# A two-block transformer kernel: 512-column up products, down products two tiles behind, and zero-padded rope scores

## What is computed

```python
h = x                                        # [256, 1024]
for i in range(2):                           # mixer 0 is MLA, mixer 1 is differential attention
    a = mixer_i(rms_norm(h, norm_g[i, 0]))
    h = h + rms_norm(a, norm_g[i, 1])
    f = conv_ffn(rms_norm(h, norm_g[i, 2]), ffn_w_up[i], ...)
    h = h + rms_norm(f, norm_g[i, 3])

def conv_ffn(x, w_up, conv_w, conv_b, w_down):   # w_up [1024, 2*2816], w_down [2816, 1024]
    u = x @ w_up
    c = conv_b + sum over j of conv_w[j] * (u shifted by j-1 tokens)     # 3 taps along the tokens
    g, val = halves of c
    return (gelu(g) * val) @ w_down

# MLA scores, 8 heads:  q_nope (128) . k_nope (128)  +  q_rope (64) . k_rope (64)
```

## Time and profile before

| what | value |
|---|---|
| time, median of 3 runs | 1247.5 us (1238.12 to 1247.79) |
| profiled execution, its own time | 1248.45 us |
| span of the profiled execution | 1246.6 us |
| PE busy | 1195.6 us, 96% |
| DVE busy | 762.8 us, 61% |
| ACT busy | 599.7 us, 48% |
| chain that ended last, PE's share | 85% |
| moved from memory | 192.84 MB, 156 GB/s over the span |

### The profile page before, as it was taken

One profiled execution on the slowest core, in us unless ns is written; L12 is line 12 of the kernel. 1 busy time (PEld: TensorE's weight loads), 2 busy tenths in 40 slices (PEclk: granted clock), 3 DMA queues, 4 the chain that ended last, 5 costly groups with the idle time before them and its releaser, 6 DMA issues.

```text
span 1246.6 us, 21628 instructions
## 1 busy us (share of the span) xinstructions
PE 1195.6 (96%) x8061; PEld 1068.2 (86%) x8075; DVE 762.8 (61%) x1066; ACT 599.7 (48%) x912; POOL 66.7 (5%) x93
## 2 busy tenths in 40 slices
PE   7999999999898989999999999999999999999997
PEld 6856999999698869999988999998887777999996
DVE  4854877776656558777767545546555556554554
ACT  5444554454555655545545443435554545443342
POOL 0201000000200010000001000001000210000000
PEclk9999999999999999999999999999998899999998
DMA  6404665666343347566655666653762014766661
GB/s 219 155 34 152 187 198 175 183 199 197 102 136 136 126 123 206 174 181 202 182 155 139 199 191 178 187 160 86 201 224 102 1 35 136 204 199 182 174 183 43
DMA packets 241059, 194.61 MB, mean 156 GB/s; under 512 B 11214, under 2 KB 223792, under 8 KB 241008
## 3 DMA queue, kind: packets, MB, share of 16 engines
q1 hardware_dynamic: 240928, 193.88, 51.8%
q10 hardware_dynamic: 80, 0.03, 0.0%
HBM read 192.84 MB, written 1.05 MB: 156 GB/s over the span
## 4 chain that ended last, share of the span: by engine, by line
PE 85%; DVE 7%; ACT 3%; DMA 2%; issue 1%; POOL 1%; SPq 0%; POOLq 0%; ACTq 0%; DVEq 0%
PE psum L572 25%; PE psum L573 25%; PE psum L574 25%; DVE lo_u L1629 1%; PE psum L1130 1%; DVE lo_u L1646 1%; ACT hi_u L1223 1%; DMA raw_u<-in_cmp_v_w 1%; PE psum L804 1%; PE psum L803 1%; PE psum L917 1%; DVE soft L1850 1%; PE psum L1087 1%; DMA raw_u<-in_mla_w_ukv 1%; DMA raw_u<-in_cmp_k_w 1%
## 5 line engine op out<-in xcount | busy, mean ns | idle before, releaser
L572 PE MATMUL psum<-act_hi,hi_u 128*128 128x256 f32 x1712 | 487.6, 285 | 7.8 <-DVE lo_u L1629 3.2
L574 PE MATMUL psum<-act_hi,lo_u 128*128 128x256 f32 x1712 | 484.9, 283 | 0.0
L573 PE MATMUL psum<-act_lo,hi_u 128*128 128x256 f32 x1712 | 484.8, 283 | 0.0
L1646 DVE TENSOR_TENSOR lo_u<-raw_u,hi_u 128x2048 fp32r<-128x2048 f32 (+3 forms) x122 | 273.7, 2243 | 244.5 <-ACT hi_u L1229 153.0
L572 PEld LDWEIGHTS psum<-act_hi,hi_u 128*128 128x128 f32 x1712 | 327.3, 191 | 16.2 <-issue 12.4
L573 PEld LDWEIGHTS psum<-act_lo,hi_u 128*128 128x128 f32 x1712 | 327.4, 191 | 3.3
L574 PEld LDWEIGHTS psum<-act_hi,lo_u 128*128 128x128 f32 x1712 | 327.4, 191 | 0.0
L1229 ACT ACTIVATE hi_u<-raw_u 128x2048 fp32r<-128x2048 f32 x72 | 137.7, 1912 | 88.6 <-PE psum L574 86.0
L572 PE MATMUL psum<-hi_d,hid_hi 128*128 128x512 f32 (+1 forms) x352 | 138.4, 393 | 1.4 <-DVE hid_lo L1736 1.4
L573 PE MATMUL psum<-lo_d,hid_hi 128*128 128x512 f32 (+1 forms) x352 | 138.0, 392 | 0.0
L574 PE MATMUL psum<-hi_d,hid_lo 128*128 128x512 f32 (+1 forms) x352 | 137.0, 389 | 0.0
(11 more groups left out here) (230 smaller groups left out, 1234.8 us busy)
## 6 DMA issues: line engine op xcount, KB each, us to landing
raw_u<-in_ffn_w_up SPq DMA_DIRECT2D x88, 512.0 KB, 5.5
raw_d<-in_ffn_w_down SPq DMA_DIRECT2D x86, 512.0 KB, 3.5
raw_u<-in_ffn_w_gu SPq DMA_DIRECT2D x84, 512.0 KB, 5.9
raw_u<-in_diff_w_qkv SPq DMA_DIRECT2D x24, 512.0 KB, 4.6
raw_u<-in_w_in SPq DMA_DIRECT2D x24, 512.0 KB, 4.0
raw_u<-in_mla_w_o SPq DMA_DIRECT2D x8, 512.0 KB, 3.7
raw_u<-in_diff_w_o SPq DMA_DIRECT2D x8, 512.0 KB, 3.7
raw_u<-in_w_out SPq DMA_DIRECT2D x8, 512.0 KB, 3.9
```

Of the source, the lines that this page charges most:

```text
L572: pe.matmul(o, s_hi, m_hi, start=start, stop=False)
L573: pe.matmul(o, s_hi, m_lo, start=False, stop=False)
L574: return pe.matmul(o, s_lo, m_hi, start=False, stop=stop)
L1646: dve.tensor_tensor(v[0], v[1], v[2].bitcast(F32), ALU.subtract).then_inc(S("lo_u_done"), 1)
```

## The change

- **Up products.** The hi and lo parts of the activations now lie side by side in `act_hl`. One 512-column matmul computes hi*hi and hi*lo at once into the two halves of a bank, and one 256-column matmul adds lo*hi to the second half (`mm_beside`). A block step is two matmuls in the place of three. The sum of the two halves is now formed outside PE: ACT copies the second half out (`cross_out`), DVE adds it to the first (`sum_up`), for the gate and for the value. What follows reads `up_sum` in SBUF and not PSUM.
- **Order on PE.** `down(t)` now runs behind `up(t+2)`, where it ran behind `up(t+1)`. At the end of an FFN the four half blocks of tiles 20 and 21 alternate.
- **Order on ACT and DVE.** The down rows that are split in a tile's turn are other ones: before, turn t split rows t+1 on both engines; now ACT splits rows t at the end of turn t, and DVE forms the lo part of rows t-1 near the start of turn t, behind the first `sum_up`. The fp32r copy of the hidden product moves from DVE to ACT, and its lo part moves into the next turn of DVE. A third slot of `hi_d` and `lo_d` holds the rows of tile 21.
- **MLA.** `m_qr` and `m_kr` get 128 partitions; the upper 64 are set to zero by two memsets at the program's start, and L804 becomes a matmul with 128 rows.
- SP's program and POOL's are the same as before.

```diff
-        act_hi = sb("act_hi", [P, KC, SEQ], F32R)
-        act_lo = sb("act_lo", [P, KC, SEQ], F32R)
+        act_hl = sb("act_hl", [P, KC, 2, SEQ], F32R)
+        act_hi, act_lo = act_hl[:, :, 0, :], act_hl[:, :, 1, :]
...
-        hi_d = sb("hi_d", [P, 2, 1024], F32R)
-        lo_d = sb("lo_d", [P, 2, 1024], F32R)
+        hi_d = sb("hi_d", [P, 3, 1024], F32R)
+        lo_d = sb("lo_d", [P, 3, 1024], F32R)
...
+        cross = ar(2048, 2, 2, SEQ)
+        up_sum = ar(3072, 2, 2, SEQ)
+        def d_slot(d):
+            return 2 if d % FT == FT - 1 else d % 2
...
-        m_qr = ar(2048, H, SEQ, p=ROPE)
+        m_qr = ar(2048, H, SEQ)
...
-        m_kr = ar(8192, SEQ, p=ROPE)
+        m_kr = ar(8192, SEQ)
...
+            def mm_beside(bank, n, s_hi, s_lo, m_hl, start, stop):
+                pe.matmul(psum[0:n, bank, :], s_hi, m_hl.rearrange("p a t -> p (a t)"), start=start, stop=False)
+                return pe.matmul(psum[0:n, bank, SEQ:], s_lo, m_hl[:, 0, :], start=False, stop=stop)
...
-                        if f < 2:
-                            pe.wait_ge(S("tap_b"), g * 2 - 2)
-                        else:
-                            pe.wait_ge(S("hid_hi_done"), g - 1)
+                        pe.wait_ge(S("up_sum"), g * 2 - 2)
...
-                        mm = mm3(psum[0:n, 4 + 2 * slot + s, 0:SEQ], hi[:, k, :], lo[:, k, :],
-                                 act_hi[:, k, :], act_lo[:, k, :], k == 0, k == KC - 1)
+                        mm = mm_beside(4 + 2 * slot + s, n, hi[:, k, :], lo[:, k, :], act_hl[:, k],
+                                       k == 0, k == KC - 1)
                         if k == KC - 1:
                             mm.then_inc(S("gate_up" if s == 0 else "used_u"), 1)
...
                 up(1, 1, P)
-                down(0, 0, P)
                 with pe.Fori(0, LOOPED) as b:
                     up(b * 2 + 2, 0, P)
+                    down(b * 2, 0, P)
+                    up(b * 2 + 3, 1, P)
                     down(b * 2 + 1, 1, P)
-                    up(b * 2 + 3, 1, P)
-                    down(b * 2 + 2, 0, P)
                 up(20, 0, P)
+                down(18, 0, P)
+                up(21, 1, width(f, 21))
                 down(19, 1, P)
-                up(21, 1, width(f, 21))
-                down(20, 0, P)
+                down(20, 0, P, False, [0])
                 down(21, 1, width(f, 21), True, [0])
+                down(20, 0, P, False, [1])
                 down(21, 1, width(f, 21), True, [1])
...
+                pe.wait_ge(S("m_rope_zeros"), 2)
...
+                    def cross_out(part):
+                        if n < P or part:
+                            act.wait_ge(S("used_u"), at(u + 1))
+                        else:
+                            act.wait_ge(S("gate_up"), at(g + 1 - (f == 3)))
+                        act.activation(cross[:, slot, part, :], psum[:, 4 + 2 * slot + part, SEQ:], ACT.Copy)\
+                            .then_inc(S("cross_out"), 2 if n < P else 1)
+                    def conv_mid(part, buf):
+                        act.wait_ge(S("up_sum"), at2(2 * g + part + 1))
...
+                    cross_out(0)
+                    if f < 2:
+                        conv_mid(0, cg)
+                        cross_out(1)
+                        act.wait_ge(S("tap_b"), at2(2 * g + 1))
+                        act.activation(gg[0:n, slot, :], cg[0:n, slot, :], ACT.Gelu_apprx_tanh).then_inc(S("gated"), 1)
+                        conv_mid(1, cv)
                     else:
...
+                        act.wait_ge(S("up_sum"), at2(2 * g + (2 if n < P else 1)))
                         r = slice(n, 2 * n) if n < P else slice(0, P)
...
+                        act.activation(gg[r, slot, :], up_sum[0:n, slot, 0, :], ACT.Silu).then_inc(S("gated"), 1)
+                        if n == P:
+                            cross_out(1)
                     if b is not None:
                         split_u_looped(b, u + 2)
                     elif t < 20:
                         split_u(u + 2)
...
-                        split_d(g + 1, b)
-                split_d(FT * f)
+                    act.wait_ge(S("hidden"), at(g + 1))
+                    if b is not None or g >= 2:
+                        act.wait_ge(S("used_d"), at(g - 1))
+                    act.activation(hid_hi[0:n, slot, :], hf[0:n, slot, :], ACT.Copy).then_inc(S("hid_hi_done"), 1)
+                    if t + 1 < FT:
+                        split_d(g, b)
+                    if t == 20:
+                        split_d(g + 1)
...
+                slot = d_slot(d) if b is None else d % 2
                 dve.wait_ge(S("hi_d_done"), d + 1 if b is None else b * 2 + (d + 1))
-                dve.tensor_tensor(lo_d[:, d % 2, :], raw_d[:, d % 2, :], hi_d[:, d % 2, :].bitcast(F32),
+                dve.tensor_tensor(lo_d[:, slot, :], raw_d[:, d % 2, :], hi_d[:, slot, :].bitcast(F32),
                                   ALU.subtract).then_inc(S("lo_d_done"), 1)
...
+                    def sum_up(part):
+                        last = n < P
+                        dve.wait_ge(S("cross_out"), at2(2 * g + (2 if last else part + 1)))
+                        dve.tensor_tensor(up_sum[:, slot, part, :], psum[:, 4 + 2 * slot + part, 0:SEQ],
+                                          cross[:, slot, part, :], ALU.add).then_inc(S("up_sum"), 2 if last else 1)
+                    def taps(part, buf):
+                        for tap, name in ((0, "tap_a"), (2, "tap_b")):
+                            dve.wait_ge(S("conv_mid" if tap == 0 else "tap_a"), at2(2 * g + part + 1))
...
+                    def hidden_low(x, slot, n):
+                        dve.wait_ge(S("hid_hi_done"), at(x + 1))
+                        dve.tensor_tensor(hid_lo[0:n, slot, :], hf[0:n, slot, :], hid_hi[0:n, slot, :].bitcast(F32),
+                                          ALU.subtract).then_inc(S("hid_lo_done"), 1)
+                    sum_up(0)
+                    if b is not None or 0 < t < 21:
+                        split_d(g - 1, b)
                     if f < 2:
...
+                        taps(0, cg)
+                    if n == P:
+                        sum_up(1)
+                    if b is not None or t:
+                        hidden_low(g - 1, 1 - slot, P)
+                    dve.wait_ge(S("gated"), at(g + 1))
+                    if f < 2:
+                        taps(1, cv)
+                        dve.wait_ge(S("tap_b"), at2(2 * g + 2))
...
+                    dve.tensor_tensor(hf[0:n, slot, :], gate, val, ALU.mult).then_inc(S("hidden"), 1)
                     if b is not None or t < 20:
                         split_u(u + 2, b)
...
-                        split_d(g + 1, b)
-                split_d(FT * f)
+                    if t == 20:
+                        split_d(g)
+                        split_d(g + 1)
+                    if t == 21:
+                        hidden_low(g, slot, n)
...
+            dve.memset(m_qr[ROPE:], 0.0).then_inc(S("m_rope_zeros"), 1)
+            dve.memset(m_kr[ROPE:], 0.0).then_inc(S("m_rope_zeros"), 1)
```

More of the change, by code:

```diff
@@ L336, in program @@
         d_sq = junk[:].rearrange("p (b d) -> p b d", d=P)
-        d_hi, d_lo = (x[:].rearrange("p a (c t) -> p (a c) t", t=SEQ) for x in (hi_d, lo_d))
+        d_hi, d_lo = (x[:, 0:2].rearrange("p a (c t) -> p (a c) t", t=SEQ) for x in (hi_d, lo_d))
         n_q = ar(0, 4, SEQ)
@@ L691, in down @@
                     g = t + FT * f
+                    d = 2 if isinstance(t, int) and t == FT - 1 else slot
                     pe.wait_ge(S("hi_d_done"), g + 1)
@@ L699, in down @@
                             mm = mm3(psum[:, 2 * tk + c, :], hid_hi[0:n, slot, tok(tk)], hid_lo[0:n, slot, tok(tk)],
-                                     hi_d[0:n, slot, w], lo_d[0:n, slot, w], False, last)
-                    mm.then_inc(S("used_d" if TT - 1 in tiles else "first_part"), 1)
+                                     hi_d[0:n, d, w], lo_d[0:n, d, w], False, last)
+                    if TT - 1 in tiles:
+                        mm.then_inc(S("used_d"), 1)
+                    elif last:
+                        mm.then_inc(S("first_part"), 1)
                 up(0, 0, P, True)
@@ L1236, in split_d @@
                 elif d >= 2:
-                    act.wait_ge(S("used_d"), d - 1)
-                act.activation(hi_d[:, d % 2, :], raw_d[:, d % 2, :], ACT.Copy).then_inc(S("hi_d_done"), 1)
+                    act.wait_ge(S("used_d"), d - 1 - (d % FT == FT - 1))
+                act.activation(hi_d[:, d_slot(d) if b is None else d % 2, :], raw_d[:, d % 2, :], ACT.Copy)\
+                    .then_inc(S("hi_d_done"), 1)
             def norm(i):
@@ new lines, in tile @@
+                    if n == P:
[6 more added lines that the diff above has]
+                        dve.wait_ge(S("tap_b"), at2(2 * g + 2))
+                        gate, val = gg[0:n, slot, :], cv[0:n, slot, :]
+                    else:
```

(12 more changed lines are left out.)

61 lines of the change are left out of this document (16 added, 45 removed).

## The result

| | before | after |
|---|---|---|
| median | 1244.4 us (4 executions, 1238.1 to 1247.8) | 1635.0 us (4 executions, 1630.2 to 1641.4) |
| ratio, 95% interval | | 1.316 [1.312, 1.320] |
| profiled execution, its own time | 1248.45 us | 1630.16 us |
| span | 1246.6 us | 1628.4 us |
| FFN 0, first `up` to last `down` | 189.1 us | 287.9 us |

The changed kernel is 31.6% slower. From the page of the changed kernel: the engines, the chain that ended last by engine, two of the costliest groups (busy, mean ns | idle before, releaser) and two kinds of transfer.

What follows compares the result with a forecast made beforehand. PE bounds the kernel before, at 8.5 us a tile; after the change a ring through the load does, at 13.6 us. 1248.45 + 401 (FFNs) - 5.5 (MLA) + 1 (later stages) = 1645 us, 8 in 10 within 1580 to 1715.

Steps and rivals of the forecast that it cites:

- head: Stretch of each FFN ahead of the first round, from the first `up` through the first `lo_d`: about 15 us.
- one round: From one `lo_d` end to the next in the FFN loop: 13.6 us per tile, 18 rounds per FFN.
- tail: Stretch of an FFN behind `lo_d` of rows 18: 29 us in FFN 0 and 1, 26 us in 2 and 3.
- the four FFNs' growth: Time added to the FFNs together: 2 x 99.9 + 2 x 100.4 = 401 us.
- stages behind the FFNs: Stages after the FFNs get their loads later, since SP reaches them behind down rows 21: 0 to 3 us.
- The ring: FFN loop: `lo_d`, load, up unit's splits, `sum_up` and the next `lo_d` in series, 13.6 us per tile.
- The weighing of the transfers: FFN loads: 7.6 us from SP's issue until the up unit lands, preferred over a page's 5.6 us estimate.
- Loads in time: Rival: the FFN loads come in time and the kernel is faster, 1233 us; chance 0.05.
- Quicker load: Rival: the load is quicker when less else goes on, ring about 1.3 us shorter, 1551 us; chance 0.08.
- Slow clock: Rival: PE's clock falls to 1.2 GHz and PE becomes the bound, 15.4 us a tile, 1775 us; chance 0.05.
- I take the upper: Up products: of bounds 0 and 17.5 us of PE time saved, 17.5 was chosen, outside the sum.
- 347 ns in turns: Sign in PE's up products: a 512- and a 256-column matmul in turns take 347 ns, where three took 360.

Runs made afterwards that it cites:

- number 1: The changed kernel with SP's order alone altered, the up unit of tile t+1 issued ahead of the down rows of tile t: 1231.8 us, ratio 0.991.
- number 7: The kernel before with one edit on DVE, lo of down rows t-1 formed near the start of turn t: 1725.0 us, ratio 1.389.
- number 10: number 1 again with more executions, on the chip of number 9: 1229.3 us, ratio 0.990.
- number 5: The changed kernel with the second transfer of each looped up unit cut to one of its eight row blocks: 1515.9 us, ratio 1.220.
- number 4: The changed kernel, loads in its own order, with the block step of three 256-column matmuls: 1632.8 us, ratio 1.317.
- number 2: number 1 with the 512-column product split in two, so three 256-column products per block step: 1236.1 us, ratio 0.995.
- number 9: number 1 with the eight 512-column products of a gate or value first, then its eight 256-column ones: 1223.7 us, ratio 0.984.
- number 6: The changed kernel with ACT and DVE splitting down rows t inside turn t, ahead of the split of unit t+2: 1356.5 us, ratio 1.092.

## Why the prediction was right

The forecast was 1645 us, the profiled execution took 1630.2, and its mechanism was shown from both sides: taking the late `lo_d` out of the load's way removes the loss (number 1), and putting it there makes the loss in the kernel before (number 7). PE's timeline of the changed kernel in FFN 0, then in FFN 3, gives their lengths, 287.9 and 283.7 us:

```profile
121.67 0.47 PE L584 MATMUL psum<-act_hl,hi_u 128*128 128x512 f32 x1 [0.31 <-DVE act_hl L1702]
...
409.15 0.39 PE L580 MATMUL psum<-hi_d,hid_lo 128*128 128x512 f32 x1
...
1336.88 0.47 PE L584 MATMUL psum<-act_hl,hi_u 128*128 128x512 f32 x1 [0.31 <-DVE act_hl L1702]
...
1620.20 0.39 PE L580 MATMUL psum<-hi_d,hid_lo 64*128 64x512 f32 x1
```

Term by term, for FFN 0 where it isn't said otherwise:

| term | predicted | measured |
|---|---|---|
| head, first `up` to the end of the first `lo_d` | 15 us | 136.71 - 121.67 = 15.0 us |
| one round | 13.6 us | (379.75 - 136.94) / 18 = 13.5 us |
| of it, `raw_d` issued to `hi_u` started | 7.7 us | 7.2 and 7.5 us in the two turns shown, 7.6 in the mean of 18 |
| tail | 29 us | 409.54 - 379.68 = 29.9 us |
| FFN 0, FFN 3 | 289, 286 us | 287.9, 283.7 us |
| the four FFNs' growth | 401 us | 98.8 + 98.7 + 98.9 + 98.3 = 394.7 us |
| MLA | -5.5 us | -5.4 us |
| stages behind the FFNs | +1 us | -7.6 us |

The ring in the two turns of the timelines was 13.3 us, in the whole of FFN 0 13.5, in FFN 3 (1596.35 - 1350.63) / 18 = 13.7. The tail went as foretold: the down rows 21 were issued behind `lo_d` of rows 19, and tile 21's `sum_up` stood behind their lo part. What the sum had too much is 6 us in the FFNs, 1 to 2 in each (in FFN 3 the head took 13.5 and the tail 24.3 us for 15 and 26, and the rounds 0.9 more), and 8.6 us behind them. Of the latter 6.7 us are one place between FFN 2 and FFN 3, and nothing of the change: it is the clock (last section).

The weighing of the transfers held: the 7.7 us from the issue to ACT's start were 7.6 in the mean of FFN 0 and 7.7 in FFN 3, in single turns 7.0 to 8.9. The 5.6 us estimated from the Trainium skill, "DMA: Bandwidth & Descriptors", section "Anatomy of one DMA", are too few for it; but the section gives its formula for one transfer that GpSimd issues, and this load is three transfers that SP issues, so the runs don't test the formula. The same page's "Rules for kernel authors" say to issue a transfer early, compute, and wait for it late; numbers 1 and 7 show what that is worth in this kernel, 403 and 483 us.

The rivals. *Loads in time* was priced at 1233 us; number 1, in which they are in time, took 1231.8 and 1229.3. That agreement is in part luck: of its terms, the 17.5 us for the products were 9.7, and the 8 us at the heads and tails about 3, since the four FFNs took 742.2 us in number 10 and 749.0 in the kernel before. *Quicker load* didn't happen, but number 5 showed that its lever is real, 1.65 us a round. *Slow clock*: behind the 4.52 us of idle time PE's steps are 0.64 us apart (206.22 to 206.86), which is (512 + 256) columns at 1.2 GHz, and from 211 us they are 0.35 us apart; the tile ahead of it, which began at 191.69 us behind 2.71 us of idle time, has 0.35 us from its start. The stretch of 190 to 217 us had a granted clock of 0.87:

```profile
190.00:217.00 27.00, 19.99 (x88) 16.47 (x88) 13.86 (x21) 11.11 (x18) 0.00 (x0) 0.87 0.40 117
```

So there is a slow stretch of 6 us in one of these two tiles, and it costs nothing, as was expected: PE is still idle 7 of the 27 us, and number 4 showed that more PE time makes nothing later.

Where a size was off: "I take the upper" for the up products, 17.5 us of PE time, not part of the sum. Of the signs that the prediction lists, its 347 ns in turns are the one that didn't come: they are 352. Both rows had the same surplus per matmul, but both were rows of one kind in a row. In turns the saving is 9.7 us (number 10 against number 2); only with the kinds kept apart does it come to 9.7 + 5.8 = 15.5 us of the 17.5 (number 9, in which tile 0 and the half tile keep the turns). The 3.5 us estimated from the Trainium skill, "TensorE: Matmul & The Clock Gate", section "Wait — 56ns, not 53.3ns?", are too few against either.

## What to carry to other kernels

In a queue that works in order, a wait costs nothing as long as nothing behind it is needed soon; so when an instruction that raises a semaphore is moved later, go through the queue that waits for it and ask of every transfer behind the wait who needs it, and in which turn. If that is the same turn, a ring has closed, and its length is a sum that can be worked out from the trace of before: here 13.6 us for 13.5 to 13.7 measured, and in number 7 14.9 for 14.8. Long waits in a table tell neither that there is such a ring nor that there is none: look at the end of the chain, whether a transfer's landing has a waiter. And moving an instruction back is not the inverse of a change when its neighbours have moved too: number 6 undid the load's ring and closed another, in the two FFNs with taps.
